# A late half of the first expert unit in the rows of h, with the saved rows and the norm's parameter rows issued by SyncE behind it

## The chip, the cores and the metric

The kernel runs on one core of a Trainium2 chip. Time is device time of one execution in microseconds (us), median of several runs. An execution profiled by the hardware gives the trace; its span runs from the first to the last instruction of the program and is a little shorter than the device time.

TensorE (PE in the profile) does the matrix products, VectorE (DVE), ScalarE (ACT) and GpSimd (POOL) the rest; SyncE (SP) only issues transfers. A transfer is cut into packets for the core's 16 DMA engines. SP, ACT and POOL each put their transfers into a queue of their own (q1, q10 and q0 in the profile); the 16 engines serve all three.

## What is computed

Two decoder layers over 256 tokens of 1024 numbers, all in float32. Each layer has a mixer and then a mixture of experts:

```python
for l in range(DEPTH):                                   # DEPTH = 2
    mix = hybrid_mixer(h, w_in[l], w_out[l], ...)        # attention, gating and convolution branches
    h = layer_norm(DEEPNORM_ALPHA * h + mix, ln_mix_g[l], ln_mix_b[l])
    ffn = grouped_moe(h, w_router, router_bias, w_gate[l], w_up[l], w_down[l])
    h = layer_norm(DEEPNORM_ALPHA * h + ffn, ln_ffn_g[l], ln_ffn_b[l])

# in grouped_moe: 16 experts, each token goes to 2 of them
    y = (jax.nn.silu(hf @ w_gate[e]) * (hf @ w_up[e])) @ w_down[e]
    out = out + gates[:, e:e + 1] * y
```

## The kernel before

**Weights as a stream.** All weights come as units of 128 partitions x 4096 float32, 16 KB in each partition and 2.10 MB together. A layer has 55: seven slabs for the mixer (five of `w_in`, two of `w_out`) and 48 for the experts, which are worked on in 8 pairs of 6 units (four of gate and up, two of down). Two layers are 110 units, 231 MB. SP issues them in order in `load_slab` and `load_experts`.

**Where a unit lies.** `ring` has 9 slots. A unit may be loaded when PE has used the unit that lay in its slot; PE counts that on the semaphore `used`, and SP waits for it at L505. Expert units are numbered k = 0 to 47 in a layer. Units 9 and 10 (`EXTRAS`) have no slot: they go to `extra[0]` and `extra[1]`, over areas that the mixer no longer needs (`area_a` and `uv`). So when the experts begin, units 0 to 10 are loaded or on their way, and unit 11 is the first that must wait for a slot freed by an expert unit: for unit 0, used by PE in the first quarter of pair 0.

**How the norm behind the mixer reaches the experts.** DVE writes the centred rows `normal` over `mix` (`norm_center`, L1405), block 0 first and block 1 last. ACT then copies them rounded to `n_hi` (L1109), which lies over `uv`, and stores them to the DRAM tensor `normal_rows` (L1110). DVE takes the rest, `first_lo` (L1597). PE gathers the tokens of pair 0 by 32 products of 128x128, 16 with `n_hi` and 16 with `first_lo` (`first_pair`, L684). The pairs after it are gathered by POOL with an indirect transfer out of `normal_rows` (`rows_of_pair`, L1315), and PE turns these rows (L718). POOL makes the rows of h out of `normal` with the norm's gain and shift (`gain_and_shift`, L1284 and L1287), reading `ln_par`, which ACT has loaded at L1034 behind its last split of `w_out`; then it scales h (L1351).

**SP's order between mixer and experts**, in both layers: unit 7, unit 8 (each when its slot of `w_out` is free), the last 4 KB per partition of unit 9 when `w_out` is used up (`chunk_used`), the second half of unit 10, and its first half only when PE has gathered pair 0 (`gathered`), since `n_hi` lies there. Then unit 11.

**The order of PE** is the program's: router, a few products with `ones_bf` that only keep PE busy (`keep_clock`, L557), `first_pair`, then for each pair `gate_up` (L747), the rows of the next pair (L718) and `down` (L770), with the products that add a pair's result back (L796) between them.

## Time and profile before

| | before |
|---|---|
| median of 3 runs | 642.38 us (641.94 to 643.33) |
| the profiled execution | 642.98 us |
| its span | 640.9 us |
| PE busy | 618.2 us (96%) |
| DVE, ACT, POOL busy | 304.0, 211.2, 148.5 us |
| bytes moved by DMA | 246.72 MB, mean 385 GB/s |

Busy time says how long an engine had work in hand. The profile also has a view of stretches (for each, every engine's busy time, PE's granted clock, the share of time in which the 16 DMA engines moved packets, and GB/s), a timeline, and the chain of waits, followed back from the last instruction. A DMA share of 1.00 means that all 16 had packets. PE's clock is granted in full in every stretch shown here.

### The profile page before, as it was taken

The numbers are of one execution on the slowest core, as the hardware profiler recorded it, in microseconds if no ns is written. First come the engines' busy times: TensorE is split into PE (matmuls) and PEld (weight loads), VectorE is DVE, ScalarE is ACT, GpSimd is POOL, SyncE is SP. The second block draws the span as 40 slices with busy tenths as digits, with TensorE's granted clock in tenths as the row PEclk, the third lists the DMA queues.
The fourth block names the chain that finished last, engine by engine and source line by source line (L and its number), as shares of the span: only waits on it lengthen the run. The fifth ranks groups of instructions, "written<-read, shape, count | busy, mean of one in ns | idle before, by whom it ended". The sixth has DMA issues, their size and how long they took to land.

```text
span 640.9 us, 8180 instructions
## 1 busy us (share of the span) xinstructions
PE 618.2 (96%) x3239; PEld 333.0 (52%) x3239; DVE 304.0 (47%) x623; ACT 211.2 (33%) x469; POOL 148.5 (23%) x139
## 2 busy tenths in 40 slices
PE   8999999999999999997999999999999999999893
PEld 5887886434344344342488878763344344344231
DVE  6899897222142141130578988871042141231226
ACT  5832964232032032030194268352032032031111
POOL 1999300620000000000049971007000000000000
PEclk9999999999999999999999999999999999999997
DMA  8999399899999999999998646989999999999991
GB/s 357 432 424 399 129 423 415 316 431 429 427 424 426 427 424 429 425 425 427 431 428 360 235 197 275 419 333 398 431 422 430 425 427 426 428 425 427 430 389 70
DMA packets 21498, 246.72 MB, mean 385 GB/s; under 512 B 3244, under 2 KB 3372, under 8 KB 6352
## 3 DMA queue, kind: packets, MB, share of 16 engines
q1 hardware_dynamic: 17712, 234.46, 87.2%
q10 hardware_dynamic: 1728, 7.87, 3.1%
q0 software_dynamic: 2016, 3.82, 1.6%
q8 instruction: 28, 0.46, 0.3%
q14 instruction: 14, 0.11, 0.0%
HBM read 246.51 MB, written 3.15 MB: 390 GB/s over the span
## 4 chain that ended last, share of the span: by engine, by line
PE 79%; DMA 12%; DVE 7%; issue 1%; ACT 1%; DVEq 0%
PE bank L747 28%; PE bank L770 15%; PE bank L639 13%; DMA ring<-in_units 11%; PE bank L796 4%; PE bank L613 4%; PE bank L852 2%; DVE w_split L1459 2%; PE bank L864 2%; PE bank L718 2%; PE bank L684 1%; PE bank L627 1%; PE bank L757 1%; PE bank L934 1%; PE bank L567 1%
## 5 line engine op out<-in xcount | busy, mean ns | idle before, releaser
L747 PE MATMUL bank<-ring,xe_pair 128*64 128x512 f32 x992 | 217.3, 593 | 7.9 <-DMA ring<-in_units 7.9
L747 PEld LDWEIGHTS bank<-ring,xe_pair 128*64 128x64 f32 x992 | 70.3, 137 | 151.0 <-issue 134.8
L1688 DVE TENSOR_TENSOR area_b<-area_b,bank 128x512 f32<-128x512 f32 x16 | 11.0, 687 | 207.2 <-PE bank L747 207.2
L770 PE MATMUL bank<-ring,area_b 128*64 128x512 f32 x480 | 107.0, 596 | 1.6 <-DVE area_b L1690 1.6
L1315 POOL DMA_INDIRECT rows<-normal_rows,tiny_i x14 | 14.4, 1026 | 265.3 <-DVE tiny_i L1638 242.4
L1299 POOL TENSOR_TENSOR in_lo<-ring,in_hi 128x512 fp32r<-128x512 f32 x56 | 71.7, 1327 | 12.3 <-ACT in_hi L1062 12.3
L1145 ACT ACTIVATE area_b<-bank 128x512 f32<-128x512 f32 x16 | 9.6, 597 | 185.7 <-PE bank L747 185.7
L770 PEld LDWEIGHTS bank<-ring,area_b 128*64 128x64 f32 x480 | 32.8, 137 | 66.9 <-issue 59.0
L1123 ACT ACTIVATE xe_pair<-bank,small 128x128 f32<-128x128 f32 x128 | 46.3, 468 | 45.0 <-PE bank L718 35.6
L1266 POOL TENSOR_TENSOR rstd<-var_eps,tiny 128x1 f32<-128x1 f32 x18 | 10.6, 593 | 194.6 <-DVE var_eps L1391 194.6
L1709 DVE SCALAR_TENSOR_TENSOR y_lo<-bank,tiny,y_hi 128x512 fp32r<-128x512 f32 x32 | 24.0, 751 | 59.7 <-ACT y_hi L1158 59.7
L1158 ACT ACTIVATE y_hi<-bank,tiny 128x512 fp32r<-128x512 f32 x32 | 22.0, 687 | 89.4 <-PE bank L770 89.4
L1767 DVE SCALAR_TENSOR_TENSOR bank<-mix,small,bank 128x256 f32<-128x256 f32 x116 | 45.6, 481 | 0.0
L639 PE MATMUL bank<-in_hi,xi_hi 128*128 128x512 f32 x112 | 44.0, 393 | 0.0
L639 PE MATMUL bank<-in_lo,xi_hi 128*128 128x512 f32 x112 | 43.7, 390 | 0.0
L639 PE MATMUL bank<-in_hi,xi_lo 128*128 128x512 f32 x112 | 43.6, 389 | 0.0
L613 PE MATMUL bank<-w_split,x_hi 128*128 128x512 f32 x128 | 39.9, 393 | 0.9 <-DVE w_split L1459 0.7
L1662 DVE TENSOR_TENSOR h<-h,bank 128x512 f32<-128x512 f32 x60 | 37.2, 680 | 1.8 <-PE bank L796 1.8
L1062 ACT ACTIVATE in_hi<-ring 128x512 fp32r<-128x512 f32 x56 | 30.0, 625 | 21.7 <-PE bank L639 18.9
L796 PE MATMUL bank<-y_hi,back 128*128 128x512 f32 x64 | 28.5, 445 | 0.0
L613 PEld LDWEIGHTS bank<-w_split,x_hi 128*128 128x128 f32 x128 | 23.7, 188 | 7.0 <-DVE w_split L1459 1.6
L796 PE MATMUL bank<-y_lo,back 128*128 128x512 f32 x64 | 25.3, 395 | 0.0
(208 smaller groups left out, 794.3 us busy)
## 6 DMA issues: line engine op xcount, KB each, us to landing
ring<-in_units SPq DMA_DIRECT2D x105, 2048.0 KB, 20.3
ln_par<-in_ln_rows ACTq DMA_DIRECT2D x4, 1024.0 KB, 11.4
extra<-in_units SPq DMA_DIRECT2D x4, 1024.0 KB, 7.8
extra<-in_units SPq DMA_DIRECT2D x2, 1536.0 KB, 20.1
ring<-in_units SPq DMA_DIRECT2D x2, 1024.0 KB, 8.1
normal_rows<-mix ACTq DMA_DIRECT2D x4, 512.0 KB, 7.0
h<-in_x SPq DMA_DIRECT2D x2, 512.0 KB, 4.0
piece_area<-in_branch_rows ACTq DMA_DIRECT2D x2, 512.0 KB, 7.4
```

Source lines behind the costliest of these rows:

```text
L613: mm = pe.matmul(bank[4 + 2 * b + n][:, :], x[:, k0, b * P:(b + 1) * P], w[:, part, :], start=k0 == 0 and k == 0, stop=k0 == KC - 1 and k ...
L639: mm = pe.matmul(dst[:, :], x[:, c, b * P:(b + 1) * P], w, start=c == 0 and k == 0, stop=c == KC - 1 and k == 2)
L747: mm = pe.matmul(bank[2 + m][e * SLOTS:(e + 1) * SLOTS, :], x[:, k, at + e * SLOTS:at + (e + 1) * SLOTS], w[:, c, m, e, :], start=k == 0, ...
L770: mm = pe.matmul(bank[5 + n][e * SLOTS:(e + 1) * SLOTS, :], hidT[:, k, e * SLOTS:(e + 1) * SLOTS], w[:, k, e, :], start=k == 0, stop=k == ...
L796: mm = pe.matmul(bank[banks[k]][:, :], back[:, b, :], part[:, n * BANK:(n + 1) * BANK], start=part is y_hi and not rows_in_bank, stop=part ...
L1062: act.activation(in_high(l, i)[:, :], unit_at(n)[:, i % KC * BANK:(i % KC + 1) * BANK], ACT.Copy)\
L1123: act.activation(dst, src, ACT.Identity, scale=col_par[:, 2 * l + 1, 0, c:c + 1], bias=col_par[:, 2 * l + 1, 1, c:c + 1]).then_inc(s["xe"], 1)
L1158: act.activation(y_hi[:, n * BANK:(n + 1) * BANK], bank[5 + n][:, :], ACT.Copy, scale=slot_gate[:, j % 2:j % 2 + 1]).then_inc(s["y_hi"], 1)
L1299: pool.tensor_tensor(in_low(l, i), ring[:, at, cols], in_high(l, i)[:, :].bitcast(F32), ALU.subtract).then_inc(in_lo_ready, 1)
L1662: dve.tensor_tensor(a, a, bank[COMB_BANKS[j % 2][k]][:, :], ALU.add).then_inc(s["added"], 1)
L1709: dve.scalar_tensor_tensor(out=y_lo[:, half], in0=bank[5 + n][:, :], scalar=slot_gate[:, j % 2:j % 2 + 1], in1=y_hi[:, half].bitcast(F32), ...
L1767: ins = dve.scalar_tensor_tensor(out=(conv if k == TAPS - 1 else sums)[:, cb, :], in0=src, scalar=tap, in1=sums[:, cb, :], op0=ALU.mult, o ...
```

## The change

The rows of h are free from the moment at which DVE has centred them and PE has turned them (`norm_ready`, `strips_pe`) until POOL writes them again. The change uses them for half a unit:

- Unit 0 of the experts is split. Its second half goes to its slot as before. Its first half is loaded late, to `expert_half` over the rows of h. The free half of the slot takes the first half of unit 11 at once, with a semaphore of its own, so of unit 11 only the second half waits for PE.
- The late half is issued in SP's queue behind unit 8 and ahead of the rest of unit 9, after a wait for `norm_ready` and `strips_pe`. Behind it SP issues the two stores to `normal_rows` (before: ACT).
- `n_hi` and `first_lo` are not made for the first gather; PE gathers pair 0 from `normal` itself, by 16 products in full float32, chunk by chunk. With nothing over `uv`, unit 10 is one transfer without the wait for `gathered`.
- `ln_par` is loaded by SP behind unit 10 (before: by ACT, ahead of unit 8).
- POOL's `gain_and_shift` waits for PE's first products with the late half (`first_half_used`), where it waited for `first_lo`.

```diff
@@ load_experts
                     if k == EXTRAS[0]:
+                        sp.wait_ge(norm_ready, TB * (l + 1))
+                        sp.wait_ge(strips_pe, TB * (l + 1))
+                        sp.dma_start(expert_half[:, :], units[l, SLABS, :, 0:HALF]).then_inc(first_half_landed, 16)
+                        for b in range(TB):
+                            sp.dma_start(normal_rows[l][b * P:(b + 1) * P, :], normal[:, b, :]).then_inc(normal_saved, 16)
                         sp.wait_ge(chunk_used, 2 * KC * (l + 1))
                         sp.dma_start(extra[0][:, EARLY:], src[:, EARLY:]).then_inc(extra_landed[0], 16)
                         continue
                     if k == EXTRAS[1]:
-                        sp.dma_start(extra[1][:, UNIT // 2:], src[:, UNIT // 2:]).then_inc(extra_landed[1], 16)
-                        sp.wait_ge(main_sems["gathered"], CHUNK_PAIRS * (l + 1))
-                        sp.dma_start(extra[1][:, 0:UNIT // 2], src[:, 0:UNIT // 2]).then_inc(extra_landed[1], 16)
+                        sp.dma_start(extra[1][:, :], src).then_inc(extra_landed[1], 16)
+                        sp.wait_ge(h_ready, 2 * TB * l + TB)
+                        sp.dma_start(ln_par[:, :, :].rearrange("p i n -> p (i n)"), bcast_row(ln_rows[1 + 2 * l], 2 * D)).then_inc(par_in, 16)
                         continue
...
-                    sp.dma_start(unit_at(n), src).then_inc(landed[n % RING], 16)
+                    if k in (0, FIRST_FREED):
+                        sp.dma_start(unit_at(n)[:, HALF:], src[:, HALF:]).then_inc(landed[n % RING], 16)
+                    else:
+                        sp.dma_start(unit_at(n), src).then_inc(landed[n % RING], 16)
+                    if k == 0:
+                        sp.dma_start(unit_at(n)[:, 0:HALF], units[l, SLABS + FIRST_FREED, :, 0:HALF])\
+                          .then_inc(freed_half_landed, 16)
@@ experts (PE)
-                def first_pair(part):
+                def first_pair():
                     for b in range(TB):
                         wait_pick(b)
-                        pe.wait_ge(n_hi_ready if part is n_hi else n_lo_ready, TB * l + b + 1)
-                        for c in range(KC):
+                    for c in range(KC):
+                        for b in range(TB):
                             mm = pe.matmul(bank[FIRST_BANKS[c // 2]][:, c % 2 * P:(c % 2 + 1) * P],
-                                           part[:, b, c * P:(c + 1) * P], first_pick[:, b, :],
...
+                                           normal[:, b, c * P:(c + 1) * P], first_pick[:, b, :],
+                                           start=b == 0, stop=b == TB - 1)
@@ scalar, gpsimd
-                act.activation(n_hi[:, b, :], normal[:, b, :], ACT.Copy).then_inc(n_hi_ready, 1)
-                act.dma_start(normal_rows[l][b * P:(b + 1) * P, :], normal[:, b, :]).then_inc(normal_saved, 16)
...
-                act.wait_ge(h_ready, 2 * TB * l + TB)
-                load_ln_rows(1 + 2 * l)
...
-                pool.wait_ge(n_lo_ready, TB * (l + 1))
+                pool.wait_ge(first_half_used, l + 1)
```

The queue of SP between the mixer and the experts, layer 0, before (a row is one transfer or several alike; `extra_121` is the place of unit 9, `extra_122` that of unit 10, and in brackets stands the semaphore waited for):

```order
L506 DMA ring<-in_units 128x4096
L506 DMA ring<-in_units 128x4096 [waits used] x6
L510 DMA extra_121<-in_units 128x3072 [waits probT_pe]
L506 DMA ring<-in_units 128x4096 [waits used] x2
L494 DMA extra_121<-in_units 128x1024 [waits chunk_used]
L497 DMA extra_122<-in_units 128x2048
L499 DMA extra_122<-in_units 128x2048 [waits moe_gathered]
L506 DMA ring<-in_units 128x4096 [waits used] x37
```

And after (`extra_122` is now unit 9, `extra_123` unit 10):

```order
L515 DMA ring<-in_units 128x2048
L519 DMA ring<-in_units 128x2048
L517 DMA ring<-in_units 128x4096 [waits used] x6
L524 DMA extra_122<-in_units 128x3072 [waits probT_pe]
L517 DMA ring<-in_units 128x4096 [waits used] x2
L498 DMA expert_half<-in_units 128x2048 [waits strips_pe,norm_ready]
L500 DMA normal_rows<-mix 128x1024 x2
L502 DMA extra_122<-in_units 128x1024 [waits chunk_used]
L505 DMA extra_123<-in_units 128x4096
L507 DMA ln_par<-in_ln_rows 128x2048 [waits h_ready]
L515 DMA ring<-in_units 128x2048 [waits used]
L517 DMA ring<-in_units 128x4096 [waits used] x36
```

The rest of unit 9 and all of unit 10 now stand behind a transfer that waits for the norm; before, they stood directly behind unit 8.

PE at the start of the experts, layer 0, before:

```order
L557 MATMUL bank<-ones_bf 128x512 x4
L684 MATMUL bank<-first_pick,n_hi 128x128 [waits n_hi_ready,moe_pick]
L684 MATMUL bank<-first_pick,n_hi 128x128 x7
L684 MATMUL bank<-first_pick,n_hi 128x128 [waits n_hi_ready,moe_pick]
L684 MATMUL bank<-first_pick,n_hi 128x128 x7
L684 MATMUL bank<-first_pick,first_lo 128x128 [waits n_lo_ready,moe_pick]
L684 MATMUL bank<-first_pick,first_lo 128x128 x7
L684 MATMUL bank<-first_pick,first_lo 128x128 [waits n_lo_ready,moe_pick]
L684 MATMUL bank<-first_pick,first_lo 128x128 x7
```

And after:

```order
L571 MATMUL bank<-ones_bf 128x512 x4
L700 MATMUL bank<-first_pick,mix 128x128 [waits moe_pick,norm_ready]
L700 MATMUL bank<-first_pick,mix 128x128 x15
L724 MATMUL bank<-tiny_b,mark_126 128x1 [waits moe_mark,casts]
L724 MATMUL bank<-tiny_b,mark_126 128x1
L767 MATMUL bank<-expert_half,xe_pair_118 64x512 [waits moe_xe,first_half_landed,landed7]
L767 MATMUL bank<-expert_half,xe_pair_118 64x512 x3
```

PE's 32 products become 16, and its first products of pair 0 wait for the late half as well.

## Rows read from the trace of the kernel before

**Rows 1.** The page: busy time of PE, its share and its instructions.

```profile
PE 618.2 (96%) x3239; PEld 333.0 (52%) x3239; DVE 304.0 (47%) x623; ACT 211.2 (33%) x469; POOL 148.5 (23%) x139
```

**Rows 2.** Timeline of PE, end of each layer's experts: start, length, group, [idle before].

```profile
272.38 3.65 PE L747 MATMUL bank<-ring,xe_pair 128*64 128x512 f32 x16 [0.26 <-DMA ring<-in_units]
...
301.76 1.51 PE L747 MATMUL bank<-ring,xe_pair 128*64 128x512 f32 x6 [1.25 <-DMA ring<-in_units]
...
603.79 3.65 PE L747 MATMUL bank<-ring,xe_pair 128*64 128x512 f32 x16 [1.03 <-DMA ring<-in_units]
...
613.57 2.80 PE L747 MATMUL bank<-ring,xe_pair 128*64 128x512 f32 x12 [1.24 <-DMA ring<-in_units]
```

**Rows 3.** Stretches of the experts: busy times, clock, DMA share, GB/s.

```profile
150.00:250.00 100.00, 100.00 (x492) 39.85 (x490) 25.68 (x48) 21.47 (x53) 3.96 (x4) 1.00 1.01 426
```

**Rows 4.** Timeline: transfers issued by SP and ACT around the start of the experts.

```profile
95.87 0.34 ACTq L1034 DMA_DIRECT2D ln_par<-in_ln_rows  x1
...
100.17 0.33 SPq L506 DMA_DIRECT2D ring<-in_units  x1
...
104.72 0.33 SPq L494 DMA_DIRECT2D extra<-in_units  x1
...
116.13 0.33 SPq L499 DMA_DIRECT2D extra<-in_units  x1
...
119.77 20.27 SPq L506 DMA_DIRECT2D ring<-in_units  x6
...
413.30 0.33 SPq L506 DMA_DIRECT2D ring<-in_units  x1
```

**Rows 5.** Stretches around the start of the experts, layer 0, then layer 1.

```profile
76.00:100.00 24.00, 23.52 (x154) 19.75 (x152) 22.57 (x32) 14.68 (x25) 0.00 (x0) 1.00 0.98 400
...
114.00:117.00 3.00, 3.00 (x27) 2.41 (x28) 2.18 (x9) 1.53 (x5) 0.00 (x0) 1.00 0.27 109
117.00:119.00 2.00, 2.00 (x12) 0.70 (x10) 0.69 (x3) 1.98 (x5) 0.68 (x1) 1.00 0.96 266
119.00:124.00 5.00, 5.00 (x26) 1.72 (x24) 0.00 (x0) 0.67 (x1) 4.88 (x3) 1.00 0.99 344
...
389.00:413.00 24.00, 23.56 (x154) 19.79 (x153) 22.70 (x32) 14.81 (x25) 0.00 (x0) 1.00 0.98 400
...
427.00:430.00 3.00, 3.00 (x26) 2.50 (x27) 2.18 (x8) 1.42 (x5) 0.00 (x0) 1.00 0.30 120
430.00:432.00 2.00, 2.00 (x12) 0.72 (x10) 0.80 (x3) 1.98 (x6) 0.00 (x0) 1.00 0.85 221
432.00:437.00 5.00, 5.00 (x26) 1.62 (x24) 0.00 (x0) 0.77 (x1) 4.75 (x3) 1.00 0.91 338
```

**Rows 6.** The quarter microsecond in which the first packets after the idle stretch appear.

```profile
117.00:117.25 0.25, 0.25 (x4) 0.12 (x2) 0.25 (x2) 0.25 (x2) 0.00 (x0) 1.00 2.20 328
```

**Rows 7.** Timeline of DVE: block 1 of the norm, layer 0 and layer 1.

```profile
107.72 0.81 DVE L1405 TENSOR_SCALAR mix<-h,mv,rstd 128x1024 f32<-128x1024 f32 x1
...
420.84 0.81 DVE L1405 TENSOR_SCALAR mix<-h,mv,rstd 128x1024 f32<-128x1024 f32 x1
```

**Rows 8.** The chain of waits in order of time: start, length, group.

```profile
112.50 3.60 PE bank L684 x32
...
154.52 0.87 PE bank L718 x8
...
324.02 7.14 PE bank L852 x32
```

**Rows 9.** Timeline of POOL, layer 0; then the page's transfers of gathered rows.

```profile
119.56 2.36 POOL L1284 TENSOR_TENSOR h<-mix,ln_par 128x1024 f32<-128x1024 f32 x1
...
135.28 1.09 POOL L1315 DMA_INDIRECT rows<-normal_rows,tiny_i  x1 [3.22 <-DVE tiny_i L1638]
...
rows<-normal_rows,tiny_i POOLq DMA_INDIRECT x14, 10.5
```

More of the change, by code:

```diff
@@ L55 @@
 EXTRAS = (RING, RING + 1)
-EXTRA_LOADS = (2, 2)
 EARLY = 3072
+HALF = UNIT // 2
+FIRST_FREED = RING + len(EXTRAS)
 RING_UNITS = LAYER_UNITS - len(EXTRAS)
@@ L676, in landed_unit @@
                     return ring[:, at, :]
-                def first_pair(part):
+                def first_pair():
                     for b in range(TB):
                         wait_pick(b)
-                        pe.wait_ge(n_hi_ready if part is n_hi else n_lo_ready, TB * l + b + 1)
-                        for c in range(KC):
+                    for c in range(KC):
+                        for b in range(TB):
                             mm = pe.matmul(bank[FIRST_BANKS[c // 2]][:, c % 2 * P:(c % 2 + 1) * P],
-                                           part[:, b, c * P:(c + 1) * P], first_pick[:, b, :],
-                                           start=b == 0 and part is n_hi and c % 2 == 0, stop=b == TB - 1 and part is first_lo,
-                                           skip_group_check=True)
-                            if b == TB - 1 and part is first_lo and c % 2 == 1:
-                                mm.then_inc(s["gathered"], 1)
+                                           normal[:, b, c * P:(c + 1) * P], first_pick[:, b, :],
+                                           start=b == 0, stop=b == TB - 1)
+                        if c % 2 == 1:
+                            mm.then_inc(s["gathered"], 1)
                 def gather(p):
@@ L736, in gate_up @@
                     for u in range(4):
-                        w = landed_unit(PAIR_UNITS * j + u).rearrange("p (c m e n) -> p c m e n", c=2, m=2, e=2)
+                        unit = landed_unit(PAIR_UNITS * j + u)
+                        halves = [unit[:, 0:HALF], unit[:, HALF:]]
+                        if ps.main and j == 0 and u == 0:
+                            pe.wait_ge(first_half_landed, 16 * (l + 1))
+                            halves[0] = expert_half[:, :]
+                        w = [part.rearrange("p (m e n) -> p m e n", m=2, e=2) for part in halves]
                         for c, m in (((0, 0), (0, 1), (1, 0), (1, 1)) if u < 3 else ((0, 0), (1, 0), (0, 1), (1, 1))):
@@ L801, in experts @@
                 if ps.main:
-                    first_pair(n_hi)
-                    first_pair(first_lo)
+                    first_pair()
                     number(1, bank[7][:, 0:1]).then_inc(first_numbered, 1)
```

32 lines of the change are left out of this document (14 added, 18 removed).

## The prediction

> **What bounds the kernel now.** The page comes first: PE is busy for 618.2 of 640.9 us [rows 1]. That reads as a kernel bound by PE, so the next question is what fills the rest. The timeline of PE at the end of each layer's experts answers it: PE waits for units to land, five times in layer 0 (0.26, 0.44 and three times about 1.24 us, 4.4 us in all) and three times in layer 1 (1.03, 1.24, 1.24; 3.5 us) [rows 2]. Until then PE lives on what was loaded ahead; from there to the layer's end each unit comes when the transfers bring it. In between the 16 DMA engines are never idle: share 1.01, 426 GB/s [rows 3], which is 4.92 us for a unit of 2.10 MB.
>
> So each layer's experts end at a time that the stream of transfers sets. A microsecond that the stream loses around the start of the experts is a microsecond of the total. One that it wins comes back too, up to the waits of 4.4 and 3.5 us. Work of PE is free within these same waits. The stretch to study is therefore the one where the stream stops, around the start of the experts.
>
> **Where the stream loses time before.** Against 426 GB/s, layer 0 loses [rows 5]: 3 - 3 x 109/426 = 2.23 us in the stretch 114 to 117, where all that was issued has run out; 2 - 2 x 266/426 = 0.75 us in 117 to 119, where the first half of unit 10 (issued at 116.13 [rows 4]) starts; 5 - 5 x 344/426 = 0.96 us in 119 to 124, where unit 11 (issued at 119.77 [rows 4]) starts. Sum 3.9 us. Layer 1 in the same way: 2.15 + 0.96 + 1.03 = 4.15 us [rows 5].
>
> The same rows give the price of a start. From the issue at 116.13 to the first packets at 117.0 [rows 4, 6] pass 0.9 us, and the first packets are slow (0.75 us lost), together 1.6 us until it is as if the stream ran in full.
>
> **What the change adds to the stream.** Bytes: none. 1.05 MB of unit 11 (2.46 us) is loaded ahead, and 1.05 MB of unit 0 moves from early to late. The gain hoped for is that these 2.46 us fill the loss above. What counts is whether the stream has something to do at each moment, so I walk along it in layer 0.
>
> Unit 7's end. From 76 to 100 the stream moves 24 x 0.400 = 9.60 MB [rows 5]. Issued for that time are units 1, 2, 6, 7 and 3072 of 4096 columns of unit 9, 9.96 MB, and `ln_par`, 1.05 MB (issued at 95.87 [rows 4]). So before, unit 7 and `ln_par` are through at 100 + 1.41/0.426 = 103.3. With `ln_par` moved behind unit 10, unit 7 is through at 103.3 - 2.46 = 100.8.
>
> First new gap. Unit 8 is still issued at 100.17 [rows 4], when a slab of `w_out` is used up; it runs from 100.17 + 1.6 = 101.8. Loss 1.0 us. It ends at 106.7.
>
> Second new gap. Before, the rest of unit 9 follows at 104.72 [rows 4]. Now the head of SP's queue is the late half, waiting for block 1 of the norm, which ends at 107.72 + 0.81 = 108.53 [rows 7]; with 0.1 us for SP (PE's gather ended at 116.10 and SP issued what waited for it at 116.13 [rows 4, 8]) it is issued at 108.6 and runs from 110.2. All of units 9 and 10 that is left is queued behind it, also both stores of `normal_rows` and `ln_par`, though their places were free at 104.7. Loss 3.5 us.
>
> After that the queue is full: 1.05 + 1.05 + 0.52 + 2.10 + 1.05 = 5.77 MB, 13.5 us, to 123.7. The second half of unit 11 is issued at about 119.8 as before, so neither the stop at 114 nor the slow starts behind it remain. Small packets of gathered rows cost a little more among full queues; I take 0.1 us.
>
> Sum for layer 0: 1.0 + 3.5 + 0.1 - 3.9 = +0.7 us. For layer 1: 24 x 0.400 MB again up to 413 [rows 5], unit 7 through at 413.8, unit 8 issued at 413.30 [rows 4] and running from 414.9, loss 1.1; it ends at 419.8; the norm ends at 421.65 [rows 7], the late half runs from 423.3, loss 3.5; 1.1 + 3.5 + 0.1 - 4.15 = +0.5 us. **Together about +1.1 us**, with an error of some 0.5 us in each of the four gaps. The half unit does fill the old hole; the waiting in front of it opens one of the same size some microseconds earlier.
>
> **A rule against the row.** The first packets come 0.9 us after the issue, and 1.6 us are lost with the slow ones [rows 4 to 6]. The Trainium skill (DMA: Bandwidth & Descriptors, section Specifications) gives about 0.6 us to the first byte for SP's transfers. By that figure alone each of the four starts would cost 1.0 us less, and the sum would be an estimated -2.9 us; the second rival has its chance.
>
> **PE.** Its 32 products of `first_pair` take 3.60 us [rows 8], 0.112 each. Full float32 is in the trace at 256 columns: the row of L852 has 32 records for 16 products in 7.14 us [rows 8], so 0.446 us a product, and 0.223 at 128 columns if it goes with the columns. 16 of them take 3.57 us: no change; bounds 3.3 (weights loaded faster) and 7.1 us (a product as dear as at 256 columns). `n_hi` was there in time before, so no wait of PE goes. Even +3.6 us would lie within the 4.4 and nearly within the 3.5 us of waits [rows 2], and unit 11's second half is no longer urgent. The Trainium skill (FP8 and Floating Point Precision, section TensorE Precision Notes) says that true FP32 takes four passes through the array; with half as many products, that would speak against this change only if the reduced form took one pass at this size, and an estimate by it alone is 3.60 us becoming 7.2. The rows give no such doubling. Taken: 0.
>
> The late half must land before PE's first product of pair 0 at 112.50 + 3.60 = 116.1 [rows 8]: 110.2 + 2.46 = 112.7, and with an estimated microsecond to land 113.7. It does, with 2 us to spare; that is also its cover if the norm came later.
>
> **POOL and ACT.** The stores run from 112.7 to 115.1, and POOL's gather for pair 1 waits for PE's until 116.1 anyway, so it goes at about 118 as before (POOL's next product stands at 119.56 [rows 9]). `ln_par` lands at about 124.5, so POOL's first product, at 119.56 before [rows 9], starts 5 us later; its four passes (2.36 us each [rows 9]) end near 134. The gather for pair 2 stands behind them and goes from 135.28 [rows 9] to about 138 to 140, lands 10.5 us later [rows 9], near 149, and PE turns these rows at 154.5 [rows 8]. Hidden, with about 4 us of cover; beyond that PE's waits of 4.4 us would take it. ACT loses two copies and three issues, DVE two subtractions, all while PE was on `first_pair` or had other work. 0.
>
> **The rivals.**
> *The lag of single engines survives (slower).* In the stretch 114 to 117 the share is only 0.27 [rows 5]: a few of the 16 engines still work on what is left while the others stand. A unit counts when its last part lands, so the old hole cost the latest engine little, perhaps 0.8 us, and it wiped out its lag. The new gap comes earlier, and what an engine falls behind afterwards, while queues are full, stays until the layer ends. The price is between 0 and the 2.2 us of that tail for each layer; it decides from the point at which the latest engine is over half a microsecond behind in the new order. At 1 us a layer the time is 642.4 + 1.1 + 2.0 = 645.5.
> *The starts are cheaper (faster).* If a transfer issued while others still run starts at once, the first gap of each layer is nothing (-2.1), and if the late half costs 0.9 instead of 1.6 that is -1.4 more: 642.4 + 1.1 - 3.5 = 640.0. The old row at 119 to 124, where unit 11 follows directly on unit 10 and still loses 0.96 us, speaks against it.
> *The half unit counts in full (faster).* 2 x 2.46 = 4.9 us, 637.5. This needs a stream that is still busy at 108.6. It has nothing left from 106.7 on.
> *The parameter rows come too late.* If POOL's rows for pair 2 hold up PE by more than its later waits, 646. It takes over 8 us of delay.
>
> **How the numbers follow.** The profiled execution took 642.98 us, 0.6 over the median of 642.38, its span 640.9; the sum is a difference between the same stretches and is put on the median: 642.4 + 1.1 = 643.5. A measurement here tells about 0.2% (1.3 us) from no change, and the forecast lies just inside. Chances: forecast, within -1.3 and +1.3, 0.46; lag or somewhat larger gaps 0.36; late parameter rows 0.03; cheaper starts 0.12; the full half unit 0.03. Faster 0.15, same 0.46, slower 0.39. The range takes in half of the cheaper starts and most of the lag: 640.8 to 646.3.
>
> **What would show it.** Right: in the profile after, unit 8 issued at 100.2 and the late half at 108.6; a stretch of some 3 us with hardly any packets before 110; a share of 1.00 from 111 to 124, where 0.27 stood; L700 at 3.6 us; PE's waits at the layers' ends longer by 0.5 to 1 us each. Wrong: a stream that has packets between 107 and 110, or waits for units at the layers' ends shorter by 2 us, or PE waiting at the first product of pair 0 for `expert_half`.

## The result and the profile after

| | before | after |
|---|---|---|
| median of 5 runs each, on one chip | 641.94 us (641.75 to 643.33) | 646.00 us (645.56 to 646.63) |
| after / before | | 1.0062, 95% interval 1.0048 to 1.0075 |
| the profiled execution, its span | 642.98, 640.9 us | 646.13, 644.4 us |
| PE busy | 618.2 us | 618.1 us |

The change costs 4.1 us (3.1 to 4.8 by the interval). PE has the same work as before, so the 4 us are waits. The timeline of PE at the end of each layer's experts shows where a good part of them is (start, length, group, [idle before <- what ended it]), layer 0 and then the last row of layer 1:

```profile
273.77 3.65 PE L767 MATMUL bank<-ring,xe_pair 128*64 128x512 f32 x16 [1.24 <-DMA ring<-in_units]
...
303.12 3.65 PE L767 MATMUL bank<-ring,xe_pair 128*64 128x512 f32 x16 [1.24 <-DMA ring<-in_units]
...
617.09 3.65 PE L767 MATMUL bank<-ring,xe_pair 128*64 128x512 f32 x16 [1.23 <-DMA ring<-in_units]
```

L767 is the old L747. The last unit that PE waits for in layer 0 comes at 303.12, before at 301.76 [rows 2]: 1.36 us later. In layer 1 it comes at 617.09, before at 613.57: 3.52 later, of which 2.16 are layer 1's own. Both layers still end at the pace of the transfers, one unit in 4.9 us; the whole train of units has moved.

What moved it stands in SP's timeline at the start of the experts:

```profile
92.24 8.46 SPq L517 DMA_DIRECT2D ring<-in_units  x2
108.74 0.33 SPq L498 DMA_DIRECT2D expert_half<-in_units  x1
109.11 0.91 SPq L500 DMA_DIRECT2D normal_rows<-mix  x2
110.07 0.92 SPq L502 DMA_DIRECT2D extra<-in_units  x1
111.03 0.78 SPq L505 DMA_DIRECT2D extra<-in_units  x1
111.85 0.53 SPq L507 DMA_DIRECT2D ln_par<-in_ln_rows  x1
120.24 0.33 SPq L515 DMA_DIRECT2D ring<-in_units  x1
```

Between unit 8 (the last of the first row, which ends at 100.70) and the late half at 108.74 SP issues nothing. The stretches over the same time (length; busy time of PE, PEld, DVE, ACT and POOL; PE's granted clock; share of the 16 DMA engines; GB/s):

```profile
100.00:103.00 3.00, 3.00 (x15) 2.49 (x14) 1.74 (x4) 0.00 (x0) 0.24 (x1) 1.00 0.87 279
103.00:107.00 4.00, 4.00 (x37) 3.33 (x39) 3.21 (x8) 1.65 (x4) 0.47 (x2) 1.00 0.93 397
107.00:110.00 3.00, 3.00 (x43) 2.08 (x36) 2.33 (x10) 1.33 (x5) 0.39 (x1) 1.00 0.30 41
110.00:114.00 4.00, 3.74 (x27) 2.08 (x25) 2.69 (x14) 0.06 (x1) 0.00 (x0) 1.00 0.82 249
114.00:117.00 3.00, 3.00 (x28) 2.70 (x28) 0.30 (x3) 2.74 (x8) 0.00 (x0) 1.00 1.01 411
117.00:119.00 2.00, 2.00 (x12) 0.72 (x10) 1.10 (x5) 1.71 (x3) 0.00 (x0) 1.00 1.22 397
119.00:124.00 5.00, 5.00 (x26) 1.69 (x24) 0.00 (x0) 0.00 (x0) 1.20 (x1) 1.00 0.92 383
```

The hole of before, 109 GB/s in 114 to 117 [rows 5], is filled (411). In its place stands a hole of 41 GB/s from 107 to 110, followed by 4 us at 249. The same stretches of before, with 396 to 451 GB/s throughout:

```profile
100.00:103.00 3.00, 3.00 (x15) 2.49 (x14) 1.75 (x4) 0.00 (x0) 0.44 (x1) 1.00 0.98 415
103.00:107.00 4.00, 4.00 (x44) 3.36 (x46) 3.40 (x8) 1.84 (x4) 0.46 (x2) 1.00 1.05 451
107.00:110.00 3.00, 3.00 (x40) 1.97 (x29) 2.33 (x12) 2.26 (x7) 0.20 (x1) 1.00 0.95 396
110.00:114.00 4.00, 3.83 (x30) 2.44 (x29) 3.31 (x12) 0.77 (x1) 0.00 (x0) 1.00 1.00 399
```

### The profile page after: what moved, and what is told of

Its sections match the earlier page's. It is cut to its first block, busy times and chain, and to the rows that moved or that the text cites. A ratio compares the mean times of both kernels' runs of the same rounds, so it can differ in the third digit from the quotient of the medians.

```text
span 644.4 us, 8170 instructions
## 1 busy us (share of the span) xinstructions
PE 618.1 (96%) x3239; PEld 333.0 (52%) x3239; DVE 300.7 (47%) x619; ACT 208.2 (32%) x465; POOL 148.3 (23%) x139
## 4 chain that ended last, share of the span: by engine, by line
PE 78%; DMA 12%; DVE 8%; issue 1%; ACT 1%; DVEq 0%
PE bank L767 28%; PE bank L792 15%; PE bank L653 13%; DMA ring<-in_units 12%; PE bank L818 4%; DVE w_split L1470 3%; PE bank L873 2%; PE bank L627 2%; PE bank L885 2%; PE bank L733 2%; PE bank L700 1%; PE bank L641 1%; PE bank L779 1%; PE bank L955 1%; DVE h L1510 1%
## 5 line engine op out<-in xcount | busy, mean ns | idle before, releaser
L767 PE MATMUL bank<-ring,xe_pair 128*64 128x512 f32 x976 | 214.0, 593 | 10.4 <-DMA ring<-in_units 10.4
L767 PEld LDWEIGHTS bank<-ring,xe_pair 128*64 128x64 f32 x976 | 69.4, 137 | 152.7 <-issue 132.5
L1277 POOL TENSOR_TENSOR rstd<-var_eps,tiny 128x1 f32<-128x1 f32 x18 | 10.6, 595 | 197.4 <-DVE var_eps L1402 197.4
```

What stands on the lines that cost most here:

```text
L767: mm = pe.matmul(bank[2 + m][e * SLOTS:(e + 1) * SLOTS, :], x[:, k, at + e * SLOTS:at + (e + 1) * SLOTS], w[c][:, m, e, :], start=k == 0, ...
```

## Experiments

What has to be told apart: is it the wait of the late half that opens the hole, what do the two other moves (the stores and `ln_par` from ScalarE to SyncE) cost alone, and does the half unit bring anything at all? Rival readings were that a stream of transfers is slower where stores and loads share a queue, and that single engines lag behind the mean.

To compare the streams of all kernels I turn the stretches into a loss, as the prediction did: length x (1 - GB/s / 426), in us, summed over three places of layer 0 (100 to 107, 107 to 114, 114 to 124 us). In the last two columns stand the start of the last expert product that waits for a unit in layer 0, and how much later that of layer 1 comes.

| kernel | time, us | ratio to before (95%) | 100:107 | 107:114 | 114:124 | layer 0 to | layer 1 |
|---|---|---|---|---|---|---|---|
| before | 642.2 | | -0.16 | 0.46 | 3.95 | 301.76 | 311.81 |
| after | 646.00 | 1.0062 (1.0048 to 1.0075) | 1.31 | 4.37 | 0.75 | 303.12 | 313.97 |
| e4_late_more | 651.12 | 1.0145 (1.0129 to 1.0160) | 1.27 | 6.29 | 1.55 | 305.48 | 316.31 |
| g4_before_params_sp | 644.67 | 1.0040 (1.0027 to 1.0053) | 1.21 | 1.51 | 3.27 | 302.45 | 313.32 |
| g3_before_stores_sp | 641.74 | 0.9994 (0.9985 to 1.0003) | 0.00 | 0.46 | 3.98 | 300.72 | 311.27 |
| e2_params_act | 640.43 | 0.9977 (0.9968 to 0.9986) | -0.07 | 3.10 | 0.78 | 300.96 | 310.85 |
| e1_stores_act | 642.28 | 1.0005 (0.9996 to 1.0014) | 1.26 | 4.00 | 0.07 | 301.52 | 312.03 |
| f5_both_act | 640.12 | 0.9967 (0.9955 to 0.9978) | -0.08 | 2.68 | 0.06 | 300.65 | 312.25 |
| f7_no_half | 644.48 | 1.0032 (1.0017 to 1.0046) | -0.09 | 0.37 | 4.49 | 301.60 | 314.71 |
| e3_tail_ahead | 642.30 | 1.0010 (0.9999 to 1.0020) | 1.21 | 1.31 | 1.32 | 300.72 | 312.05 |
| f8_ahead_stores_sp | 641.46 | 0.9994 (0.9984 to 1.0004) | -0.15 | 0.63 | 3.16 | 301.01 | 310.93 |
| g1_unit9_ahead | 640.92 | 0.9986 (0.9976 to 0.9996) | 0.04 | 1.51 | 1.15 | 299.95 | 312.53 |
| f6_best | 646.27 | 1.0066 (1.0049 to 1.0083) | -0.04 | 0.66 | 4.16 | 303.93 | 313.68 |
| g2_unit9_ahead_stores_act | 651.71 | 1.0127 (1.0092 to 1.0162) | -0.07 | 1.45 | 1.07 | 306.47 | 315.97 |

Before ran beside each group of kernels, with medians of 642.21 (e), 642.07 (f) and 642.19 us (g). A ratio is to that one; the row of after is from its own comparison, with before at 641.94. The stretches and the ends are from one profiled execution each, and such an execution lies up to 1.8 us off the median of its kernel (f5, 641.92 against 640.12), so differences of a few tenths in these columns say nothing, and in the ends not even those of 1 us say much. Against before, the end of layer 0 moves by 1.3 us less to 0.5 us more than the three losses together (f6 and g2 apart, which lose more behind 124 us): the loss is a guide to the time and no measure of it. The six executions of g2 lie in two groups, 646.41 and 646.73, and 651.55 to 653.38; the profiled one is of the second.

### The wait of the late half

**e4_late_more** is after with one more wait ahead of the late half, for a later step of the router:

```diff
                     if k == EXTRAS[0]:
+                        sp.wait_ge(mask_ready, l + 1)
                         sp.wait_ge(norm_ready, TB * (l + 1))
```

> The changed kernel with one more wait in front of the late half: SyncE waits for mask_ready as well, 2.8 us later in the trace of the changed kernel. Theory A: the empty stretch grows by 2.8 us in each layer and all of it ends in the total, plus 5 to 6 us, 651 to 652. Theory B: plus 0 to 2 us. Theory C: ln_par lands 2.8 us later, plus under 1 us as long as TensorE's waits hide it. TensorE may wait up to 0.5 us for the late half at its first product of pair 0; that is hidden by its later waits.

651.12 us, 5.1 more than after, as the first theory has it. The issues of SP in its timeline, with the stretch of the hole:

```profile
111.26 0.33 SPq L499 DMA_DIRECT2D expert_half<-in_units  x1
...
121.34 0.33 SPq L516 DMA_DIRECT2D ring<-in_units  x1
```

```profile
107.00:110.00 3.00, 3.00 (x36) 1.95 (x29) 2.36 (x11) 1.10 (x4) 0.16 (x1) 1.00 0.02 5
110.00:114.00 4.00, 3.74 (x28) 2.22 (x26) 2.46 (x12) 0.29 (x1) 0.00 (x0) 1.00 0.36 72
```

The late half is issued 111.26 - 108.74 = 2.52 us later, and layer 0 ends 2.36 us later, 0.94 us per us. In layer 1 it is issued at 428.19, in after at 423.08; less the 2.36 that layer 0 has passed on, that is 2.75 us later, and layer 1 itself takes 2.34 more, 0.85 us per us. So this wait is paid nearly in full, in each layer. One dose shows that a microsecond which the stream stands still at this place costs most of one in the total, the main step of the prediction. PE also waited 1.28 us for the half unit here, and unit 11 is issued 1.1 us later, so a part of the 2.4 us may have gone that way. The two were not separated; both follow from the late issue.

### The moves to SyncE's queue, together with the half unit

**e2_params_act** is after with `ln_par` issued by ScalarE again, ahead of unit 8:

```diff
                         sp.dma_start(extra[1][:, :], src).then_inc(extra_landed[1], 16)
-                        sp.wait_ge(h_ready, 2 * TB * l + TB)
-                        sp.dma_start(ln_par[:, :, :].rearrange("p i n -> p (i n)"), bcast_row(ln_rows[1 + 2 * l], 2 * D)).then_inc(par_in, 16)
...
+                act.wait_ge(h_ready, 2 * TB * l + TB)
+                load_ln_rows(1 + 2 * l)
```

> The changed kernel with ln_par loaded by ScalarE ahead of unit 8 again, as before the change. Theory A: its 2.46 us of transfer lie again in front of unit 8, so the empty stretch there (1.0 us) goes and the one ahead of the late half shrinks by as much as is left (1.4 us); both layers together 3 to 4.5 us back, 641.5 to 643. Theory B: the stores still slow the start of what is behind them; 1 to 2 us back, 644 to 645. Theory C: GpSimd's first product stands at 120 again, not at 128, and all of the loss goes, 642.

**e1_stores_act** is after with the two stores to `normal_rows` issued by ScalarE again, behind its part of the router:

```diff
-                        for b in range(TB):
-                            sp.dma_start(normal_rows[l][b * P:(b + 1) * P, :], normal[:, b, :]).then_inc(normal_saved, 16)
...
+                for b in range(TB):
+                    act.wait_ge(norm_ready, TB * l + b + 1)
+                    act.dma_start(normal_rows[l][b * P:(b + 1) * P, :], normal[:, b, :]).then_inc(normal_saved, 16)
```

> The changed kernel with one part undone: the two stores of normal_rows are issued by ScalarE again and not by SyncE; all else as changed. Theory A (the stream has empty stretches, of 1 us ahead of unit 8 and of 3 us ahead of the late half): the stores fill nothing that is empty, so 645.5 to 646.5. Theory B (the stores stand among reads in SyncE's queue and the reads behind them start slowly, as the stretch 118 to 120 of the changed kernel shows): 1 to 1.5 us back in each layer, 643 to 644. Theory C (the norm's parameter rows land late, so GpSimd and ScalarE hold up TensorE): no change, 646.

**f5_both_act** is after with both edits.

> The changed kernel with both moves of transfers undone: the stores of normal_rows and ln_par are issued by ScalarE as before; the late half in the rows of h, the early half of unit 11, the gather out of normal and the undivided unit 10 stay. If the prices of the two moves are separate (3.7 and 5.6 us on their own), 636.7; if they share a hole, 638 to 640.

e2 takes 640.43 us, 5.6 less than after and 1.8 less than before, with an interval that excludes no change, and less than any of its theories had. Its stretches:

```profile
100.00:103.00 3.00, 3.00 (x15) 2.46 (x14) 1.75 (x4) 0.00 (x0) 0.40 (x1) 1.00 0.98 415
...
107.00:110.00 3.00, 3.00 (x40) 1.97 (x33) 2.33 (x12) 1.19 (x5) 0.26 (x1) 1.00 0.68 205
110.00:114.00 4.00, 3.74 (x27) 2.19 (x26) 2.56 (x13) 0.19 (x1) 0.00 (x0) 1.00 0.81 262
```

The first gap is gone (415 where after has 279), and the second is less deep (205 where it has 41), since 1.05 MB of `ln_par` are in the stream while SP has nothing to issue. That is 1.38 + 1.27 = 2.65 us less of loss in layer 0, and its end comes 2.16 us earlier. The late half is issued at 108.61, within 0.13 us as in after, so the wait itself did not change; what ran out behind it did.

e1 takes 642.28 us, 3.7 less than after, outside what each of its theories gave. The size was a surprise, and the stretches explain only a part: they lose 1.1 us less in layer 0, and its end comes 1.60 earlier. Most of that stands at 114 to 124, where the old hole was: 0.07 us lost in e1, 0.75 in after; in layer 1, at 427 to 437, nothing in e1 and 1.31 in after. But f5, which has both edits, takes 640.12 us, not 3.7 below e2: 0.3, less than the spread of either. So with the half unit the stores in SP's queue cost 3.7 us when `ln_par` stands in it too, and nothing that can be told when it does not. I cannot say from the stretches why: f5's lose 1.1 us less than e2's in layer 0 as well, and its time does not show it. That the 3.7 us need both moves is shown; what they are made of stays open.

The other way round, `ln_par` moved while the stores are on ScalarE (f5 to e1) costs 2.2 us, 2.4 by the ratios. The prediction had 2.1 for that, as its two first gaps.

### The same moves without the half unit

**g4_before_params_sp** is before with `ln_par` issued by SP behind unit 10 and nothing else:

```diff
                         sp.dma_start(extra[1][:, 0:UNIT // 2], src[:, 0:UNIT // 2]).then_inc(extra_landed[1], 16)
+                        sp.wait_ge(h_ready, 2 * TB * l + TB)
+                        sp.dma_start(ln_par[:, :, :].rearrange("p i n -> p (i n)"), bcast_row(ln_rows[1 + 2 * l], 2 * D)).then_inc(par_in, 16)
...
-                act.wait_ge(h_ready, 2 * TB * l + TB)
-                load_ln_rows(1 + 2 * l)
```

> The kernel before with the other part alone: ln_par is loaded by SyncE behind unit 10 and not by ScalarE ahead of unit 8. Theory A: unit 8 finds the stream empty for 1.0 us, the stretch from 114 on is empty for longer, and the 2.46 us of ln_par then stand in front of unit 11, which starts at 122.7 and not at 121.4; 1.3 us in each layer, 644.5 (643.5 to 645.5). If moving ln_par costs only beside the half unit, 642.

**g3_before_stores_sp** is before with the two stores issued by SP, behind a wait for the norm and the second half of unit 10:

```diff
+                        sp.wait_ge(norm_ready, TB * (l + 1))
+                        for b in range(TB):
+                            sp.dma_start(normal_rows[l][b * P:(b + 1) * P, :], normal[:, b, :]).then_inc(normal_saved, 16)
                         sp.wait_ge(main_sems["gathered"], CHUNK_PAIRS * (l + 1))
...
-                act.dma_start(normal_rows[l][b * P:(b + 1) * P, :], normal[:, b, :]).then_inc(normal_saved, 16)
```

> The kernel before with one part of the change alone: SyncE issues the stores of normal_rows, behind the second half of unit 10 and ahead of its first half, after a wait for the norm. Nothing else. The read behind them is issued at 116.1 when the stream stands anyway. Theory A: 642, no change. Theory B (stores in SyncE's queue cost by themselves, wherever they stand): 643.5 to 645.5.

g4: 644.67 us, 2.5 more than before and as its first theory has it, with the interval well off no change. Two of its stretches:

```profile
100.00:103.00 3.00, 3.00 (x15) 2.49 (x14) 1.74 (x4) 0.00 (x0) 0.21 (x1) 1.00 0.88 279
...
119.00:124.00 5.00, 5.00 (x26) 1.64 (x24) 0.00 (x0) 0.88 (x1) 0.70 (x1) 1.00 1.03 428
```

With `ln_par` gone from ahead of unit 8, the same 279 GB/s as in after stand at 100 to 103, without any late half. It gives part of it back: behind unit 10 it fills 119 to 124, which lost 0.96 us before.

One might think that it costs more beside the half unit, which has filled that place already: e2 to after, it is 5.6 us and not 2.5. The runs say otherwise. With the stores on ScalarE there are four kernels, with `ln_par` in either place, and with or without the half unit and what comes with it (the gather out of `normal` and the whole unit 10):

| stores on ScalarE | `ln_par` on ScalarE | `ln_par` on SP | the move |
|---|---|---|---|
| without the half unit | before, 642.1 to 642.2 | g4, 644.67 | +2.5 |
| with it | f5, 640.12 | e1, 642.28 | +2.2 |
| what the half unit brings | -2.0 | -2.4 | |

The two changes simply add, within the noise. The rest of the slowdown is the step from e1 to after, the stores to SP's queue: 2.0 us won, 2.2 lost by the move of `ln_par`, 3.7 lost by the stores ahead of it, 3.9 in all, where after beside its own before shows 4.1. Stores and `ln_par` both on SP without the half unit were not run, so whether the 3.7 us need the half unit too stays open.

g3: 641.74 us, no change. Stores in SP's queue are free here, with `ln_par` on ScalarE.

### The half unit alone

**f7_no_half** is f5 without the half unit: unit 0 and unit 11 are whole, and unit 10 is still one transfer without its old wait, because PE gathers from `normal`.

```diff
-                        sp.wait_ge(norm_ready, TB * (l + 1))
-                        sp.wait_ge(strips_pe, TB * (l + 1))
-                        sp.dma_start(expert_half[:, :], units[l, SLABS, :, 0:HALF]).then_inc(first_half_landed, 16)
...
-                    if k in (0, FIRST_FREED):
-                        sp.dma_start(unit_at(n)[:, HALF:], src[:, HALF:]).then_inc(landed[n % RING], 16)
-                    else:
-                        sp.dma_start(unit_at(n), src).then_inc(landed[n % RING], 16)
...
+                    sp.dma_start(unit_at(n), src).then_inc(landed[n % RING], 16)
```

> As the kernel with both moves undone, but without the half unit: unit 0 whole in its slot early, unit 11 whole when PE has used unit 0, nothing in the rows of h. Unit 10 is still one transfer without a wait, and pair 0 is gathered out of normal. Unit 11 starts at 121.4 as before the change, and what lies ahead of it are the same bytes, so the stream ends as before: 642 (641 to 643). Then the half unit is worth the distance to the kernel with both moves undone, 2 x 2.46 us less what its wait costs. If the freed unit 10 or the gather were what gains, this kernel would be near that one.

644.48 us, 4.4 more than f5, but also 2.4 more than before, where 642 had been expected. Its stream runs dry at the place where the half unit would have been on its way:

```profile
117.00:119.00 2.00, 2.00 (x13) 0.59 (x10) 0.95 (x4) 1.52 (x2) 0.00 (x0) 1.00 0.24 98
119.00:124.00 5.00, 5.00 (x26) 1.71 (x24) 0.00 (x0) 0.00 (x0) 3.26 (x2) 1.00 0.65 202
```

Unit 11 is issued at 120.05, as always when the freed slot decides. So the half unit works, but not all of the 4.4 us need be its own. In f7 PE also waits for the rows of pair 1, 2.03 us at 132.34 and more in layer 1, where the timeline of PE has

```profile
445.68 1.84 PE L718 MATMUL bank<-small,rows 128*128 128x128 f32 x8 [2.38 <-DMA rows<-normal_rows,tiny_i]
```

Behind that wait the granted clock is 0.50 from 446 to 449, and the stream falls to 369 and 396 GB/s from 453 to 461. The stores of these rows take 9.6 us to land, in before 7.0 (medians of the pages); that they are slow because the whole unit 10 runs beside them is not shown. Against before, f5 wins 2.0 us, with all that comes with the half unit. Of the 2 x 2.46 = 4.9 us that its bytes are worth, between 2.0 and 4.4 arrive.

### Something ahead of the late half

If the wait is what costs, transfers that need not wait could go ahead of it. Five kernels do this, with different parts.

**e3_tail_ahead** is after with the rest of unit 9 and the second half of unit 10 issued ahead of the late half:

```diff
                     if k == EXTRAS[0]:
+                        sp.wait_ge(chunk_used, 2 * KC * (l + 1))
+                        sp.dma_start(extra[0][:, EARLY:], src[:, EARLY:]).then_inc(extra_landed[0], 16)
+                        sp.dma_start(extra[1][:, HALF:], units[l, SLABS + EXTRAS[1], :, HALF:]).then_inc(extra_landed[1], 16)
                         sp.wait_ge(norm_ready, TB * (l + 1))
...
-                        sp.wait_ge(chunk_used, 2 * KC * (l + 1))
-                        sp.dma_start(extra[0][:, EARLY:], src[:, EARLY:]).then_inc(extra_landed[0], 16)
...
-                        sp.dma_start(extra[1][:, :], src).then_inc(extra_landed[1], 16)
+                        sp.dma_start(extra[1][:, 0:HALF], src[:, 0:HALF]).then_inc(extra_landed[1], 16)
```

> The changed kernel with the rest of unit 9 and the second half of unit 10 issued ahead of the late half and not behind it (first half of unit 10 behind it). Theory A: these 1.57 MB (3.7 us) fill the empty stretch of 3 us and its slow start; 2.5 to 4 us back in each layer, 638 to 641. Theory B: under 1 us back in each layer, 644 to 646, since the stores and what is behind them stay. Theory C: ln_par lands about when it did; 646.

**f6_best** is this order with both edits of f5, **f8_ahead_stores_sp** the same with the stores left to SP behind the late half.

> As the kernel with both moves undone, and the rest of unit 9 and the second half of unit 10 stand ahead of the late half. With ln_par back in front of unit 8 the stretch ahead of the late half is only some 1.4 us and a slow start; filled, 0.5 to 1.5 us back in each layer: 634 to 636. If the filling only moves the hole, no better than with both moves undone alone.

> The kernel with both moves undone and the tail of units 9 and 10 ahead of the late half, but with the stores of normal_rows issued by SyncE behind the late half, as in the changed kernel: a stream without empty stretches around the stores. If the stores among reads cost by themselves, 3 to 4 us above the same kernel with the stores on ScalarE; if they only cost beside an empty stretch, under 1 us above it.

**g1_unit9_ahead** is e2 with the rest of unit 9 alone ahead of the late half, **g2_unit9_ahead_stores_act** the same with the stores issued by ScalarE.

> The kernel with ln_par back on ScalarE ahead of unit 8 (640.4 us; its stretch 107 to 110 has 205 GB/s), with one more step: the rest of unit 9 (0.52 MB, 1.2 us) goes ahead of the late half. Unit 8 ends near 109, so these bytes cover what is empty until the late half starts, and the late half still lands in time (at 113 to 114; TensorE needs it at 116.3). Theory A (the stream's losses count, and TensorE's start if it is touched): 0.5 to 1.2 us back in each layer, 638 to 639.5. Theory D (what is filled in front of the late half comes back as a later late half): 640.4 or more, with TensorE waiting at its first product of pair 0.

> The same step on the kernel with the stores on ScalarE too (640.1 us). The stores now share the engines with the late half, which so lands up to 2.5 us later, at 115 to 117. Theory A without such a clash: 637.5 to 639. Theory D: TensorE waits 0.5 to 1.5 us for the late half, unit 11 is freed later, 640 to 642, above the kernel with the stores on SyncE.

None of them beats e2 or f5: 642.30 (e3), 646.27 (f6), 641.46 (f8), 640.92 (g1) and 651.71 us (g2). Yet in all of them the hole at 107 to 114 is smaller (1.5 us or less lost, where e2 loses 3.10). Only e3 is faster than the kernel it was made from, after, by 3.7 us, which is less than its first theory and more than its second. f8 shows where the hole went, in its stretches and SP's next issue:

```profile
107.00:110.00 3.00, 3.00 (x40) 1.97 (x29) 2.33 (x12) 1.15 (x5) 0.22 (x1) 1.00 0.99 410
...
119.00:124.00 5.00, 5.00 (x26) 2.06 (x24) 0.00 (x0) 0.00 (x0) 2.56 (x2) 1.00 0.53 166
```

All that has room is loaded sooner, and then the stream waits for PE to free the slot of unit 0. In f8 that is 1.1 us later still (unit 11 at 121.36, in e2 at 120.10), because PE waits 1.24 us for a late half that has 1.57 MB ahead of it. In f8 the hole moves: 0.6 us are lost at 107 to 114 and 3.2 at 114 to 124. In g1 the same shows in layer 1 (1.46 us lost at 432 to 437, in e2 0.18), but in layer 0 only 0.4 of the 1.6 us come back, and why its time is no better stays open. My reading is that the size of the hole is set by how much memory is free and by when PE frees more, so that only bytes with a place of their own fill it, as the half unit's do.

f6 and g2 are far worse than f8 and g1, and they differ from these in one thing, the queue of the stores. For f6 I had expected the opposite. In f6 the stores, in ACT's queue, run beside the late half in SP's. The page gives the time from issue to landing, of f6 and then of f8:

```profile
expert_half<-in_units SPq DMA_DIRECT2D x2, 1024.0 KB, 10.2
```

```profile
expert_half<-in_units SPq DMA_DIRECT2D x2, 1024.0 KB, 8.5
```

PE waits for it 2.27 us. Its timeline and the stretches, with the granted clock as third number from the end:

```profile
118.93 3.62 PE L764 MATMUL bank<-expert_half,xe_pair 128*64 128x512 f32 x8 [2.27 <-issue]
```

```profile
116.00:118.00 2.00, 0.66 (x8) 0.56 (x6) 1.15 (x7) 1.89 (x5) 0.00 (x0) 1.00 1.02 426
118.00:120.00 2.00, 1.07 (x4) 0.55 (x6) 0.26 (x1) 0.78 (x1) 0.00 (x0) 0.76 0.86 358
120.00:122.00 2.00, 2.00 (x6) 0.60 (x5) 0.00 (x0) 0.00 (x0) 0.00 (x0) 0.50 0.08 31
122.00:124.00 2.00, 2.00 (x10) 0.79 (x8) 0.00 (x0) 0.00 (x0) 1.33 (x2) 0.89 0.01 4
```

After the idle time the clock is at half (0.50, the level of 1.2 GHz): 8 products take 3.62 us where 8 take 2.01 a little later. PE frees unit 0's slot late, unit 11 is issued at 124.31 in place of 120.1, and from 120 to 124 the DMA engines stand (31 and 4 GB/s).

g2 loses its time one step later. Its late half is in time, but its stores take 11.5 us to land (7.9 in g1), so POOL issues the gather for pair 1 at 123.74 (in g1 at 119.96) and PE waits for the rows. Timeline of POOL, timeline of PE, then two stretches of g2:

```profile
123.74 1.20 POOL L1327 DMA_INDIRECT rows<-normal_rows,tiny_i  x1 [16.27 <-issue]
```

```profile
134.37 1.33 PE L729 MATMUL bank<-small,rows 128*128 128x128 f32 x8 [3.81 <-DMA rows<-normal_rows,tiny_i]
```

```profile
136.00:138.00 2.00, 1.22 (x8) 0.82 (x8) 0.69 (x1) 2.00 (x7) 1.38 (x2) 0.50 1.00 426
...
140.00:142.00 2.00, 2.00 (x6) 0.47 (x4) 0.00 (x0) 0.00 (x0) 0.79 (x1) 0.52 0.39 86
```

Again the clock is at half after the wait, and this time the stream stops at 140. The same in layer 1, with 4.14 us of wait and 0.52 to 0.63 as the clock behind it.

Idle time of this length does not always cost the clock. In layer 1 of f6 PE waits longer than in layer 0:

```profile
434.28 1.94 PE L764 MATMUL bank<-expert_half,xe_pair 128*64 128x512 f32 x8 [2.53 <-issue]
```

The clock is 1.00 there in every stretch from 429 to 439, and still the DMA engines stand from 435 to 439 (49 and 18 GB/s). So the late freeing of the slot stops the stream by itself, and the clock adds to it in layer 0. The cover of the first pairs is thin: with transfers ahead of the late half it matters in which queue the two transfers lie that PE needs next. Without them it does not show: in f5, with the stores in ACT's queue too, the late half lands after 6.8 us, in e2 after 6.6.

## Why the prediction was right and wrong

It had said 643.5 us, +1.1, with 640.8 to 646.3 as its range; within 0.2% had 0.46 and slower 0.39. Measured are 646.0, +4.1. The direction is right and so is the gap in front of the late half; the size is too small by 2.5 us on the medians and by 3.0 as a difference. That the time lies in the range is partly luck: the range was put around a before of 642.4, and before took 641.94 beside after; as differences the range is -1.6 to +3.9, and +4.1 lies just outside. What the prediction had wrong is a term that it put at nothing: the stores in SP's queue, with `ln_par` behind them, cost 3.7 us by the runs (e1 to after).

**What bounds the kernel.** Right. PE's waits for units at the layers' ends grew from 4.4 to 5.4 us and from 3.5 to 5.0, its busy time did not change, and e4 gives 0.94 and 0.85 us of a layer for each us of delay.

**The first gap.** Its cause was right, shown by g4 alone: with `ln_par` away, the stream is empty ahead of unit 8. Taken was 1.0 us; measured are 1.31 + 0.16 = 1.47 in layer 0. In layer 1, over 401 to 420, the loss grows from 0.25 to 1.28 us, by 1.03, where 1.1 was taken. (The stretch 389 to 413 shows 375 GB/s, before 400 [rows 5], but its extra loss of 1.4 us lies wholly in 389 to 401, where layer 1 starts 1.4 us later than before and the stretch stands still; it is not counted twice.)

**The second gap.** Taken 3.5; measured 4.37 - 0.46 = 3.9 in layer 0 and 3.96 - 0.44 = 3.5 in layer 1. The late half was issued at 108.74, forecast 108.6. A fine cut of that start, in stretches of after:

```profile
108.75:109.00 0.25, 0.25 (x3) 0.10 (x1) 0.00 (x0) 0.21 (x1) 0.00 (x0) 1.00 0.00 0
...
109.50:109.75 0.25, 0.25 (x3) 0.13 (x2) 0.25 (x4) 0.00 (x0) 0.00 (x0) 1.00 1.73 164
...
110.00:111.00 1.00, 1.00 (x7) 0.39 (x4) 0.86 (x6) 0.00 (x0) 0.00 (x0) 1.00 0.61 90
111.00:112.00 1.00, 0.83 (x9) 0.34 (x8) 0.48 (x4) 0.00 (x0) 0.00 (x0) 1.00 0.82 311
```

The first packets come 0.76 us after the issue (0.9 was taken), yet at 110 to 111 there are only 90 GB/s. The Trainium skill (DMA: Bandwidth & Descriptors, section Specifications) has about 0.6 us to the first byte, and the trace nearly agrees with that; it is the slow packets after it that make a start dear, and the sum of -2.9 us that the figure alone would give is refuted by +4.1 and, with the stores left on ScalarE, by the +0.1 of e1.

**The old hole.** In the stretches this is the term that failed. All of its 3.9 and 4.15 us were to go. Gone are 3.95 - 0.75 = 3.2 us in layer 0, and in layer 1 4.15 - 1.31 = 2.8, by the stretches of layer 1:

```profile
427.00:430.00 3.00, 2.91 (x27) 2.92 (x27) 0.71 (x3) 1.61 (x4) 0.00 (x0) 1.00 0.91 322
430.00:432.00 2.00, 2.00 (x17) 1.32 (x17) 0.90 (x6) 1.83 (x5) 0.00 (x0) 1.00 1.05 426
432.00:437.00 5.00, 5.00 (x26) 1.65 (x24) 0.51 (x2) 1.06 (x1) 1.09 (x1) 1.00 1.05 377
```

"After that the queue is full" holds by the share of 0.91 to 1.05, but a full queue moved 322 and 377 GB/s here, not 426. The share says that engines have packets, not at what rate they pass. Taken for it was 0.1 us, for the small packets of gathered rows; no run shows that price. What the runs show is that the rest of the old hole goes away with the stores: e1, which has the same queue without them, loses 0.07 us in layer 0 and nothing in layer 1. The prediction counted the stores only by their bytes, and their move at nothing.

**The sums.** In layer 0 +1.47 + 3.91 - 3.20 = +2.2 us, where +0.7 was taken; in layer 1 +1.03 + 3.5 - 2.8 = +1.7, where +0.5 was. Together +3.9 us, against +4.1 measured on the medians and 1.36 + 2.16 = 3.5 by the ends in the same two traces. The terms were too small by 2.7: 1.8 of that in the two old holes, some 0.4 each in the first and the second gap of layer 0. That the sum comes so near is in part luck: from e1 to after it counts 1.1 us in layer 0 and 1.2 in layer 1 (401 to 437) for the stores, where the time has 3.7, and it has e1 1.1 us worse than before in layer 0, though its time is the same.

**The lag of single engines.** By its number, 645.5, this rival comes near, but the sum of mean losses needs no help from it: it has the ends move by more than the mean loss, and they moved by 1.36 where the mean gives 2.2, and by 2.16 where it gives 1.7. In g4 layer 0's mean loss is up by 1.8 us and its end by 0.7. There is no common sign that it asks for. Why single ends stray from the mean loss, by up to 1.3 us, is open; no run here separates the engines.

**PE.** `first_pair` took 3.81 us, forecast 3.57, before 3.60 [rows 8], from the chain:

```profile
112.77 3.81 PE bank L700 x32
...
427.11 3.81 PE bank L700 x32
```

So there was no doubling, and the 0.2 us lie within PE's later waits. The late half was in time: PE's first product with it starts at 116.54 without a wait. It takes 6.2 us from issue to landing (median of the page), so it lands near 114.9, with 1.6 us to spare where 2 had been forecast. f6 shows what this cover is worth.

**POOL.** Right in kind, too small in size: `ln_par` lands at 128.0, forecast 124.5, and the timeline of POOL has

```profile
128.08 2.36 POOL L1295 TENSOR_TENSOR h<-mix,ln_par 128x1024 f32<-128x1024 f32 x1 [7.73 <-DMA ln_par<-in_ln_rows]
...
140.85 1.09 POOL L1326 DMA_INDIRECT rows<-normal_rows,tiny_i  x1 [0.15 <-issue]
```

8.5 us later than before (119.56 [rows 9]), where 5 had been forecast. The gather for pair 2 goes at 140.85, 5.6 us later than before (135.28 [rows 9]), and PE turns its rows at 154.83 without a wait. By the 10.6 us to landing that the transfers of `rows` take in this trace (median; 11.7 at most), an estimate is that they land at 151.5, with 3.4 us to spare. So it stayed hidden, and the fourth rival was not near.

**What would have been better.** The kernel e2 (or f5, which is not told from it): the half unit with `ln_par` left where it was. It beats before by 0.23% (0.14 to 0.32) and after by 5.6 us. The prediction had a part of this in its hands: it named the first gap as the price of moving `ln_par`, rightly sized, and did not ask what would be left of the change without that move.

## What to carry to other kernels

When weights arrive as one stream, write down for each moment what the queue still holds; a transfer that waits at the head of a queue costs whatever runs out behind it, and a small independent load issued on another engine can be what keeps the stream alive. When a change has several parts, price each alone and in pairs: here two parts added up, and two others cost 3.7 us only together. Reordering a full stream may only move its hole. And before something is moved ahead of a transfer that an engine needs next, look at how much time that transfer has to spare, since a wait of 2 us and more on PE can also cost its clock.

## What the runs showed of the hardware that was not expected

- After 2.27 us without products PE's granted clock was 0.76 and then 0.50, its lower level (f6, 118 to 122), after 2.38 us 0.50 (f7, 446 to 449), after 3.81 us again 0.50 (g2, 136 to 138). After the 1.28 us of e4, the 1.24 of f8, the 2.03 of f7 and the 2.53 of f6's layer 1 it was 1.00 in the stretches read behind them. So the length of the wait alone does not decide.
- With 1.57 MB ahead of it, the late half of 1.05 MB took 8.5 us from issue to landing (f8), and 10.2 when the stores of 1.05 MB came in ACT's queue beside it (f6). Behind an empty queue it took 6.2 (after), and with the stores beside it 6.8 (f5). The stores took 11.5 us in ACT's queue beside a full stream (g2), 7.9 in SP's behind the late half (g1), and 8.3 in ACT's in f5.
- 16 products of 128x128 in full float32 (32 records in the trace) took 3.81 us, 0.24 each, and 32 of the reduced form 3.60, 0.11 each: at this size the full form is worth about two of the reduced.
- The DMA share of 1.22 in a stretch with 397 GB/s (after, 117 to 119) and of 1.05 with 377 (432 to 437): a share of 1 or more is no proof of the full rate of 426.
